# Delta rule block inverse: the four lower levels computed for the even block columns only, packed to 32 columns

## Chip, cores and metric

One NeuronCore of a Trainium2 chip runs the whole program. The metric is device time in microseconds (us) of one execution. The kernel before takes 2286.87 us, the median of three runs.

## What is computed

The reference applies two transformer blocks to a tensor `x` of 256 tokens by 2048 channels. The first block mixes tokens with a multiscale pool and with an RWKV-7 recurrence, which is a delta rule:

```python
def step(S, inp):
    r_t, w_t, k_t, v_t, a_t, b_t = inp
    sa = jnp.einsum('bhij,bhj->bhi', S, a_t)
    S = S * w_t[:, :, None, :] + sa[..., None] * b_t[:, :, None, :] + v_t[..., None] * k_t[:, :, None, :]
    y = jnp.einsum('bhij,bhj->bhi', S, r_t)
    return S, y
...
k = k * (1.0 + (a - 1.0) * k_a.astype(f32))
r_h, k_h, v_h, a_h = hs(r), hs(k), hs(v), hs(a)
y = wkv7_scan(r_h, hs(decay), k_h, v_h, -kk, kk * a_h)
```

There are 16 heads of size 64. The block goes on with `w_out`, a wide MLP (8192) and a gated embedding. The second block has a gated linear attention, a sparse attention and a SwiGLU MLP. All of it is float32.

## The kernel before

The kernel takes the recurrence in chunks of C = 64 tokens, NCH = 4 of them. Inside a chunk the dependence of each token on the earlier ones is a strictly triangular 64x64 matrix G for each head. The kernel needs the inverse of identity minus G for 16 heads x 4 chunks = 64 small matrices. Two heads share the 128 partitions: HM = 8 pairs m, with head e of a pair on partitions 0 to 63 or 64 to 127.

The inverse is built by doubling. It starts from 2x2 diagonal blocks (`level1`). Then, for block size b = 2, 4, 8, 16 (`LEVELS`, line 35), pairs of neighbouring b-blocks are joined into 2b-blocks. The last size, 32, is done apart, by `corner_group` (line 948). Names of this stage:

- `Di` (line 270) holds the inverse so far, `DTi` (line 269) its transpose.
- `Fi` (line 271) holds the intermediate product under a mask. The mask `levels` (line 57) keeps only entries whose block row is odd and whose block column is the even one just before it.
- A level works in four groups g of two pairs each. A group has 2 x 4 x 2 = 16 products of 64x64 matrices (`inverse_group`, line 931). They fill one PSUM bank as 8 x 64 columns, the two heads of a pair in the two halves of the partitions.

One level lv runs like this. TensorE makes G x Di for the four groups into the banks `INV` (line 966, `f_ready`). VectorE multiplies each bank with the mask into `Fi` (line 2377, `f_masked`). TensorE makes D x Fi for the four groups, with DTi as the stationary operand, into banks 4 and 5 in turn (line 975, `df_ready`). VectorE adds each bank to Di (line 2360, `d_added`), and turns Di into DTi (line 2309, `dt_turned`). The next level's first products wait for `d_added`, its second products for `dt_turned`. With two banks for the second products, group 2 waits until group 0 has been added.

Every engine runs its own program in order, so the order around the stage is the order of the source. Between the two sets of products TensorE has `pool_half` (line 920): 24 products of 128x256 for another part of the model, recorded at line 673 in the helper `three`. Its first use here, `pool_half(0)`, waits for a weight tile that VectorE splits in `low1(7, 2)` (line 2205). Between masks and additions VectorE has one long operation per level: `low1(7, 3)` at level 0, `mask_copied` (line 2350) at level 1, `low1(8, 0)` at level 2, `mask_copied` at level 3. A `low1` is a subtraction over 128x2048 elements.

After the levels come the corner products, a turn of v (line 944), two more `pool_half`, the copies of the corners (lines 2397 and 2402), and the sequential scan over the chunks (lines 1004 to 1041).

A float32 product stands in the trace as two pairs of LDWEIGHTS and MATMUL. So 4 levels x 8 groups x 16 products = 512 calls are 1024 records of line 937.

Of the kernel before, what the change touches and what calls it, by code (L numbers as in the profile page):

```python
# [14 lines left out]
ALU = mybir.AluOpType  # L15
# [3 lines left out]
P = 128  # L19
T = 256  # L20
# [9 lines left out]
HM = RW // P  # L30
C = 64
NCH = T // C
KAPPA = float(np.exp(-0.5))
GN_EPS = 64e-5
LEVELS = (2, 4, 8, 16, 32)
# [86 lines left out]
def build(nc, inp, consts, out):  # L122
# [46 lines left out]
    PS = ctx.enter_context(nc.psum_tensor("PS", [P, 8, 512], F32))  # L169

    S = {n: ctx.enter_context(nc.semaphore(n)) for n in SIGNALS.split()}
# [8 lines left out]
    def split(v, dims):  # L180
        if len(dims) == 2:
            return v.rearrange("p (a b) -> p a b", a=dims[0])
        if len(dims) == 3:
            return v.rearrange("p (a b c) -> p a b c", a=dims[0], b=dims[1])
        if len(dims) == 4:
            return v.rearrange("p (a b c d) -> p a b c d", a=dims[0], b=dims[1], c=dims[2])
        return v

    def area(at, *dims):
        n = int(np.prod(dims))  # L190
        assert at + n <= NA, (at, dims)
        return split(arena[:, at:at + n], dims)

    def over(ap, n):

        return ap.unsqueeze(1).broadcast_to([ap.shape[0], n, ap.shape[1]])
# [49 lines left out]
    B32 = C // 2  # L246
# [11 lines left out]
    B = 27 * ZW  # L258
# [9 lines left out]
    G = area(B, HM, 2, NCH, P)  # L268
    DTi = area(AR_AT + 4096, HM, NCH, C)
    Di = area(AR_AT + 6144, HM, NCH, C)  # L270
    Fi = area(B + 4 * 2048, HM, NCH, C)
    UVa = [area(AR_AT + 6144, 2, HM, 2, C), area(B + 4 * 2048, 2, HM, 2, C)]

    def UV(c):
# [23 lines left out]
    INV = (2, 3, 0, 1)  # L298
# [18 lines left out]
    GT = area(B + 2048, HM, T)  # L317

    XN1 = area(B, TT, D)

    gain1 = small[:, 64:80]
    RB1 = area(AR_AT + 5632, T)
# [328 lines left out]
    def _(pe):  # L651
# [227 lines left out]
        for g in range(2 * (NCH - 1)):  # L879
            c, m0 = g // 2, g % 2 * 4  # L880
            if g >= 4:
                pe.wait_ge(S["bk_copied" if g % 2 else "bk_taken"], (g - 2) // 2)
            for m in range(4):
                mm = pe.transpose(PS[:, 4 + g % 4, m * P:(m + 1) * P], BK[:, m0 + m, c, :], ident)
# [35 lines left out]
        def pool_half(x):  # L920

            pool_tile(2 + x // 2, x % 2)
# [8 lines left out]
        def inverse_group(g, bank, lhs, rhs):  # L931
            for m in range(2 * g, 2 * g + 2):
                for c in range(NCH):
                    for e in range(2):
                        h = HALF[e]
                        at = (m % 2 * NCH + c) * C
                        mm = pe.matmul(PS[h, bank, at:at + C], lhs(h, m, c, e), rhs(h, m, c, e), start=True, stop=True)  # L937
            return mm

        def turn_v(c):  # L940
# [17 lines left out]
        for lv in range(len(LEVELS) - 1):  # L958
            for g in range(4):
                if lv == 0:  # L960
                    pe.wait_ge(S["score_masked"], 2 * HM - 3 + g)
                    pe.wait_ge(S["score_copied"], 2 * g + 2)
                    pe.wait_ge(S["d_ready"], g + 1)
                else:
                    pe.wait_ge(S["d_added"], 4 * (lv - 1) + g + 1)
                inverse_group(g, INV[g], lambda h, m, c, e: G[h, m, e, c, 0:C], lambda h, m, c, e: Di[h, m, c, :])\
                    .then_inc(S["f_ready"], 1)
            pool_half(lv)
            for g in range(4):
                pe.wait_ge(S["f_masked"], 4 * lv + g + 1)  # L970
                if lv:
                    pe.wait_ge(S["dt_turned"], 4 * (lv - 1) + g + 1)
                if g >= 2:
                    pe.wait_ge(S["d_added"], 4 * lv + g - 1)
                inverse_group(g, 4 + g % 2, lambda h, m, c, e: DTi[h, m, c, :], lambda h, m, c, e: Fi[h, m, c, :])\
                    .then_inc(S["df_ready"], 1)

        for g in range(2):
# [34 lines left out]
        for c in range(NCH):  # L1013
# [4 lines left out]
            for m in range(HM):  # L1018
                for e in range(2):
                    mm = pe.matmul(PS[HALF[e], 0, m * C:(m + 1) * C], G[:, m, e, c, 0:C], UV(c)[:, m, e, :],  # L1020
                                   start=True, stop=True)
# [7 lines left out]
            for m in range(HM):  # L1029
                for e in range(2):  # L1030
                    mm = pe.matmul(PS[HALF[e], 1, m * C:(m + 1) * C], DTi[HALF[e], m, c, :], ZSB[HALF[e], m, :],
                                   start=True, stop=True)
# [5 lines left out]
            if c < NCH - 1:  # L1038
                for m in range(HM):
                    for e in range(2):  # L1040
                        mm = pe.matmul(PS[HALF[e], 2, m * C:(m + 1) * C], BKtok(c)[:, m, e * C:(e + 1) * C],
                                       UV(c)[:, m, e, :], start=True, stop=True)
# [34 lines left out]
        for t in range(TT):  # L1077
            pe.wait_ge(S["gate_copied"], t + 1)
            pe.wait_ge(S["yn_ready"], t + 1)
            for m in range(HM):  # L1080
                mm = pe.transpose(PS[:, 4 + 2 * t + m // 4, m % 4 * P:(m % 4 + 1) * P], Ytok[:, t, m * P:(m + 1) * P], ident)
# [85 lines left out]
        for n in range(N_KCVC, N_GOQ):  # L1167
# [3 lines left out]
            if n == N_KSVS:  # L1171
                pe.wait_ge(S["w_low"], NARROW)
                for k in range(KT):
                    mm = three(PS[0:SWM, 4, 0:T], (SWH[:, k, :], SW[:, k, :]), (woven(XH[:, k, :]), woven(actT[:, k, :])),
                               k == 0, k == KT - 1)
# [3 lines left out]
        for h in range(GH):  # L1179
            mm = pe.matmul(PS[:, 6 + h // 2, h % 2 * T:(h % 2 + 1) * T], GW2[:, h * P:(h + 1) * P], LR, start=True, stop=True)  # L1180
        mm.then_inc(S["low_rank"], 1)
        for t in range(TT):
            mm = pe.transpose(PS[:, 5, t * 24:t * 24 + 24], LRG[32:SWM, t * P:(t + 1) * P], ident[32:SWM, 32:SWM])
# [84 lines left out]
        for i in range(2):  # L1268
            mm = pe.matmul(PS[:, 4 + i, :], con("ones"), KSQ[:, 2 * i:2 * i + 2, :].rearrange("p a b -> p (a b)"),
                           start=True, stop=True)  # L1270
# [7 lines left out]
        for t in range(TT):  # L1278
            for h in range(GH):
                mm = pe.transpose(PS[:, 4 + t, h * P:(h + 1) * P], K4[:, h, t * P:(t + 1) * P], ident)  # L1280
# [59 lines left out]
        for i in range(2):  # L1340
            mm = pe.transpose(PS[:, 2, i * CB:(i + 1) * CB], PTAB[i], ident[0:CB, 0:CB])
# [60 lines left out]
        for kv in range(KVH):  # L1402
            mm = pe.matmul(PS[0:NB, 3, P + kv * DH:P + (kv + 1) * DH], HID[1][:, kv * NB:(kv + 1) * NB], CW2[1], start=True, stop=True)
# [64 lines left out]
        for c in range(4):  # L1468
            n = N_REST2 + c // 2
            if c >= 2:  # L1470
                pe.wait_ge(S["sum_step"], SUM["out2"] + c - 1)
            for j in (2 * (c % 2), 2 * (c % 2) + 1):
                pe.wait_ge(S["w_low"], split_count(n, j))
                wh, wl = (a.rearrange("p (k n) -> p k n", k=4) for a in (high_home(n, i, j), unit_at(n % 2, j)))
                for k in range(4):
                    for t in range(TT):
                        x, tok = 8 + j % 2 * 4 + k, slice(t * P, (t + 1) * P)
                        mm = three(pair[c % 2][:, t, :], (XH2[:, x, tok], actT[:, x, tok]),
                                   (woven(wh[:, k, :]), woven(wl[:, k, :])), x == 8, x == KT - 1)
# [37 lines left out]
    def _(act):  # L1517
# [68 lines left out]
        def first_squares(c):  # L1586

            act.wait_ge(S[X_LOADED[c]], 16)
            act.activation(XN1[:, 0, CW * c:CW * (c + 1)], xs[:, 0, CW * c:CW * (c + 1)], ACT.Square,
                           accum_out=chunk_sums[:, 0, c:c + 1]).then_inc(S["chunk_summed"], 1)  # L1590
# [11 lines left out]
        for h in range(2):  # L1602
            act.wait_ge(S["n1_dve"], 6 + h)
            copy(r32(XH1[h]), XN1[:, h, :].rearrange("p (k t) -> p k t", k=8)).then_inc(S["x1_high"], 1)

# [481 lines left out]
    def _(v):  # L2087
# [88 lines left out]
        def first_squares(c):  # L2176

            v.wait_ge(S[X_LOADED[c]], 16)
            v.tensor_tensor_reduce(out=XN1[:, 1, CW * c:CW * (c + 1)], in0=xs[:, 1, CW * c:CW * (c + 1)],
                                   in1=xs[:, 1, CW * c:CW * (c + 1)], scale=1.0, scalar=0.0, op0=ALU.mult, op1=ALU.add,  # L2180
# [15 lines left out]
        for h in range(2):  # L2196
            v.tensor_tensor(XN1[:, h, :].rearrange("p (k t) -> p k t", k=8), actT[:, 8 * h:8 * h + 8, :], over(RB1, 8),
                            ALU.mult).then_inc(S["n1_dve"], 1)
# [8 lines left out]
        for h in range(2):  # L2207
            v.wait_ge(S["x1_high"], h + 1)
            v.tensor_tensor(r32(XL1[h]), XN1[:, h, :].rearrange("p (k t) -> p k t", k=8), high_of(XH1[h]), ALU.subtract)\
                .then_inc(S["x1_low"], 1)  # L2210
# [82 lines left out]
        for e in range(2):  # L2293
            h = HALF[e]
# [21 lines left out]
        for g in range(2 * HM):  # L2316
            m, e = g // 2, g % 2
# [34 lines left out]
        def eight(a, g):  # L2352
            return a[:, 2 * g:2 * g + 2].rearrange("p m c j -> p (m c) j")

        def bank8(b):
            return PS[:, b, :].rearrange("p (q j) -> p q j", q=8)

        def block_added(lv, g):
            v.wait_ge(S["df_ready"], 4 * lv + g + 1)
            v.tensor_tensor(eight(Di, g), bank8(4 + g % 2), eight(Di, g), ALU.add).then_inc(S["d_added"], 1)  # L2360

        def block_turned(lv, g):
            v.wait_ge(S["d_added"], 4 * lv + g + 1)
# [9 lines left out]
        for lv in range(len(LEVELS) - 1):  # L2373
            mask = con("levels")[:, lv * C:(lv + 1) * C]
            for g in range(4):
                v.wait_ge(S["f_ready"], 4 * lv + g + 1)
                v.tensor_tensor(eight(Fi, g), bank8(INV[g]), over(mask, 8), ALU.mult).then_inc(S["f_masked"], 1)
            if lv == 0:
                low1(7, 3)
            elif lv == 1:  # L2380
                mask_copied(slice(0, P), slice(C, P))
            elif lv == 2:
                low1(8, 0)
            else:
                mask_copied(LO, slice(0, C))
            block_added(lv, 0)
            block_added(lv, 1)
            block_turned(lv, 0)
            block_added(lv, 2)
            block_turned(lv, 1)  # L2390
            block_added(lv, 3)
            block_turned(lv, 2)
            block_turned(lv, 3)
# [91 lines left out]
        for i in range(F1_PARTS):  # L2485
            for c in range(8):
                n = N_F1 + c
# [33 lines left out]
        for c in range(4):  # L2521
            n, r = N_GATE + c, xs[:, :, columns(c)]
# [42 lines left out]
        for c in range(4):  # L2565
            n = N_GLA + c
# [537 lines left out]
```

## Time and profile before

| | |
|---|---|
| three runs, us | 2286.87, 2286.2, 2287.71 |
| median, us | 2286.87 |
| profiled execution, span from first to last instruction, us | 2284.1 |
| TensorE matmul busy | 2262.9 us (99%) |
| TensorE weight load busy | 2054.8 us (90%) |
| VectorE busy | 1453.5 us (64%) |
| ScalarE busy | 981.0 us (43%) |
| GpSimd busy | 169.3 us (7%) |
| granted TensorE clock | 0.999 of full speed |

The profile gives one execution by its span alone. The median of the runs is 2.8 us above it, which is time before the first and after the last instruction together with the scatter between executions. In the rows below, PE is TensorE's matmuls, PEld its weight loads, DVE is VectorE, ACT is ScalarE, POOL is GpSimd. A matmul's duration reaches from its start to its modelled end and overlaps with the next ones, so that the rate of a burst is read from where it starts, where the next line starts and how many records lie between.

### The profile page before, as it was taken

The numbers are of one execution on the slowest core, as the hardware profiler recorded it, in microseconds if no ns is written. First come the engines' busy times: TensorE is split into PE (matmuls) and PEld (weight loads), VectorE is DVE, ScalarE is ACT, GpSimd is POOL, SyncE is SP. The second block draws the span as 40 slices with busy tenths as digits, with TensorE's granted clock in tenths as the row PEclk, the third lists the DMA queues.
The fourth block names the chain that finished last, engine by engine and source line by source line (L and its number), as shares of the span: only waits on it lengthen the run. The fifth ranks groups of instructions, "written<-read, shape, count | busy, mean of one in ns | idle before, by whom it ended". The sixth has DMA issues, their size and how long they took to land.

```text
span 2284.1 us, 34500 instructions
## 1 busy us (share of the span) xinstructions
PE 2262.9 (99%) x15676; PEld 2054.8 (90%) x15676; DVE 1453.5 (64%) x1214; ACT 981.0 (43%) x931; POOL 169.3 (7%) x136
## 2 busy tenths in 40 slices
PE   9999999999999999999999999999999999999999
PEld 8998988998988988988889999888998998999898
DVE  6699676664665665665558559686655665565564
ACT  5653355433333333344544364475343433433442
POOL 1004110110110110110000000100000000011000
PEclk9999999999999999999999999999999999999999
DMA  8553166656665656666556655345555655665644
GB/s 252 174 163 90 34 238 199 207 192 211 194 215 190 212 193 205 200 231 209 175 179 190 190 183 151 117 142 184 193 194 199 224 187 184 221 211 176 227 160 147
DMA packets 335306, 425.06 MB, mean 186 GB/s; under 512 B 4521, under 2 KB 249625, under 8 KB 334777
## 3 DMA queue, kind: packets, MB, share of 16 engines
q1 hardware_dynamic: 333465, 418.50, 56.2%
q0 software_dynamic: 1552, 4.23, 0.6%
q8 instruction: 123, 2.02, 0.4%
q14 instruction: 22, 0.18, 0.0%
q10 hardware_dynamic: 144, 0.13, 0.0%
HBM read 420.75 MB, written 2.10 MB: 185 GB/s over the span
## 4 chain that ended last, share of the span: by engine, by line
PE 94%; DVE 5%; ACT 1%; issue 0%; DMA 0%; DVEq 0%; SPq 0%; ACTq 0%
PE PS L673 51%; PE PS L719 23%; PE PS L721 11%; PE PS L937 1%; DVE ring_r L2205 1%; PE PS L718 1%; PE PS L738 1%; PE PS L1129 1%; PE PS L856 0%; PE PS L1200 0%; ACT arena_r L1527 0%; PE PS L1010 0%; PE PS L1065 0%; PE PS L1057 0%; PE PS L1319 0%
## 5 line engine op out<-in xcount | busy, mean ns | idle before, releaser
L1527 ACT ACTIVATE arena_r<-ring 128x2048 fp32r<-128x2048 f32 (+1 forms) x394 | 689.9, 1759 | 934.2 <-PE PS L673 536.1
L2147 DVE TENSOR_TENSOR ring_r<-ring,arena_r 128x2048 fp32r<-128x2048 f32 x316 | 721.5, 2290 | 489.9 <-ACT arena_r L1527 489.9
L719 PE MATMUL PS<-arena_r,arena_r 128*128 128x512 f32 x2432 | 789.7, 382 | 0.0
L673 PE MATMUL PS<-arena_r,arena_r 128*128 128x512 f32 (+2 forms) x2128 | 707.6, 346 | 0.9 <-DVE actT_r L2138 0.7
L721 PE MATMUL PS<-arena_r,ring_r 128*128 128x256 f32 x2280 | 621.5, 273 | 0.0
L673 PE MATMUL PS<-ring_r,arena_r 128*128 128x512 f32 (+1 forms) x1504 | 523.3, 361 | 1.2 <-DVE ring_r L2205 1.2
L719 PEld LDWEIGHTS PS<-arena_r,arena_r 128*128 128x128 f32 x2432 | 449.1, 189 | 56.2
L673 PE MATMUL PS<-arena_r,actT_r 128*128 128x512 f32 (+1 forms) x1184 | 442.1, 373 | 0.0
L721 PEld LDWEIGHTS PS<-arena_r,ring_r 128*128 128x128 f32 x2280 | 437.4, 192 | 4.0
L673 PEld LDWEIGHTS PS<-arena_r,arena_r 128*128 128x128 f32 (+1 forms) x2128 | 401.5, 189 | 42.9 <-issue 4.8
L673 PEld LDWEIGHTS PS<-ring_r,arena_r 128*128 128x128 f32 x1504 | 277.4, 190 | 35.7 <-issue 3.1
L673 PEld LDWEIGHTS PS<-arena_r,actT_r 128*128 128x128 f32 x1184 | 224.0, 189 | 30.0
L673 PE MATMUL PS<-actT_r,arena_r 128*128 128x256 f32 (+1 forms) x656 | 180.4, 275 | 0.0
L673 PE MATMUL PS<-arena_r,ring_r 128*128 128x256 f32 x640 | 176.0, 275 | 0.0
L673 PE MATMUL PS<-ring_r,actT_r 128*128 128x256 f32 x832 | 143.3, 278 | 1.6 <-DVE ring_r L2205 1.6
L673 PE MATMUL PS<-ring_r,ring_r 128*128 128x256 f32 x512 | 140.8, 275 | 0.0
L673 PEld LDWEIGHTS PS<-ring_r,actT_r 128*128 128x128 f32 x832 | 126.4, 192 | 4.2 <-DVE ring_r L2205 2.1
L673 PEld LDWEIGHTS PS<-actT_r,arena_r 128*128 128x128 f32 (+1 forms) x656 | 124.9, 190 | 0.3 <-issue 0.2
L673 PEld LDWEIGHTS PS<-arena_r,ring_r 128*128 128x128 f32 x640 | 122.9, 192 | 0.0
L3036 POOL TENSOR_TENSOR arena_r<-arena,cst 128x1024 fp32r<-128x1024 f32 x16 | 62.0, 3876 | 612.9 <-DVE arena L2509 612.9
L2540 DVE TENSOR_TENSOR ring_r<-ring,arena_r 128x1024 fp32r<-128x1024 f32 x56 | 68.4, 1235 | 50.4 <-ACT arena_r L1527 50.3
L673 PEld LDWEIGHTS PS<-ring_r,ring_r 128*128 128x128 f32 x512 | 98.3, 192 | 0.0
(381 smaller groups left out, 1639.1 us busy)
## 6 DMA issues: line engine op xcount, KB each, us to landing
ring<-in_w_ffn_up SPq DMA_DIRECT2D x32, 2048.0 KB, 9.4
ring<-in_w_ffn_down SPq DMA_DIRECT2D x32, 2048.0 KB, 7.9
ring<-in_w_in SPq DMA_DIRECT2D x22, 2048.0 KB, 8.2
ring<-in_w_gate SPq DMA_DIRECT2D x22, 2048.0 KB, 8.2
ring<-in_w_up SPq DMA_DIRECT2D x22, 2048.0 KB, 8.2
ring<-in_w_in SPq DMA_DIRECT2D x32, 1024.0 KB, 5.4
ring<-in_w_out SPq DMA_DIRECT2D x16, 2048.0 KB, 8.8
ring<-in_w_down SPq DMA_DIRECT2D x12, 2048.0 KB, 8.1
```

Of the source, the lines that this page charges most:

```text
L673: mm = pe.matmul(dst, r32(w, early)[rows], r32(x, early)[rows], start=first and q == 0, stop=last and q == 2)
L718: pe.matmul(dst[:, 0:T], r32(wl[:, k, c]), r32(high), start=False, stop=False)
L719: mm = pe.matmul(dst, r32(wh[:, k, c]), r32(beside(high, low)), start=x == 0, stop=x == KT - 1)
L721: mm = pe.matmul(dst[:, 0:T], r32(wl[:, k, c]), r32(high), start=False, stop=False)
L738: mm = pe.transpose(PS[:, 8 - banks + j % banks, q * T + t * P:q * T + (t + 1) * P], xs[:, t, k * P:(k + 1) * P], ident)
L937: mm = pe.matmul(PS[h, bank, at:at + C], lhs(h, m, c, e), rhs(h, m, c, e), start=True, stop=True)
L1129: mm = pe.matmul(PS[:, 4 + t, :], pT[:, k, t * P:(t + 1) * P], pproj[:, c, k, :], start=(k == 0), stop=(k == 1))
L1527: return act.activation(dst, src, ACT.Copy, scale=scale)
L2147: v.tensor_tensor(r32(u), u, high_of(high_home(n, i, j)), ALU.subtract).then_inc(S["w_low"], counts(units, j))
L2205: v.tensor_tensor(r32(w), w, high_of(high_at(u), True), ALU.subtract).then_inc(S["in_low"], 1)
L2540: v.tensor_tensor(r32(u), u, high_of(HIH[q % 4]), ALU.subtract).then_inc(S["w_low"], 1)
L3036: pool.tensor_tensor(r32(XD[:, 4 * c:4 * c + 4]), RQ[c % 2], one, ALU.mult).then_inc(S["ffn1_high"], 1)
```

## The change

The mask of a level leaves nothing in the odd block columns. The changed kernel therefore computes only the even block columns of both products, 32 of 64, and packs them beside each other:

- The moving operand of the first products is a strided view of Di: blocks of b columns, every other one (`even`). Its stationary operand, G, stays 64x64.
- The masks read 8 x 32 columns of PSUM and write a packed `FE` of 32 columns a matrix at the place of `Fi`.
- The second products have `FE` as the moving operand, 32 columns; the stationary operand DTi stays 64x64.
- The additions change the even block columns of Di alone.

The number of instructions, their order on every engine, and all waits stay as they were. The turns of Di into DTi, the pool products and the long VectorE operations are unchanged, as is the corner step.

```diff
+    FE = area(B + 4 * 2048, HM, NCH, C // 2)
...
+    def even(ap, b):
+
+        names = {2: "p", 3: "p q", 4: "p m c"}[len(ap.shape)]
+        return ap.rearrange(f"{names} (n s b) -> {names} n s b", s=2, b=b)[..., 0, :]
...
-                        at = (m % 2 * NCH + c) * C
-                        mm = pe.matmul(PS[h, bank, at:at + C], lhs(h, m, c, e), rhs(h, m, c, e), start=True, stop=True)
+                        at = (m % 2 * NCH + c) * B32
+                        mm = pe.matmul(PS[h, bank, at:at + B32], lhs(h, m, c, e), rhs(h, m, c, e), start=True, stop=True)
...
-                inverse_group(g, INV[g], lambda h, m, c, e: G[h, m, e, c, 0:C], lambda h, m, c, e: Di[h, m, c, :])\
+                inverse_group(g, INV[g], lambda h, m, c, e: G[h, m, e, c, 0:C],
+                              lambda h, m, c, e: even(Di[h, m, c, :], LEVELS[lv]))\
                     .then_inc(S["f_ready"], 1)
...
-                inverse_group(g, 4 + g % 2, lambda h, m, c, e: DTi[h, m, c, :], lambda h, m, c, e: Fi[h, m, c, :])\
+                inverse_group(g, 4 + g % 2, lambda h, m, c, e: DTi[h, m, c, :], lambda h, m, c, e: FE[h, m, c, :])\
                     .then_inc(S["df_ready"], 1)
...
+        def even8(b, lv):
+            return PS[:, b, 0:T].rearrange("p (q n b) -> p q n b", q=8, b=LEVELS[lv])
+
         def block_added(lv, g):
             v.wait_ge(S["df_ready"], 4 * lv + g + 1)
-            v.tensor_tensor(eight(Di, g), bank8(4 + g % 2), eight(Di, g), ALU.add).then_inc(S["d_added"], 1)
+            d = even(eight(Di, g), LEVELS[lv])
+            v.tensor_tensor(d, even8(4 + g % 2, lv), d, ALU.add).then_inc(S["d_added"], 1)
...
-                v.tensor_tensor(eight(Fi, g), bank8(INV[g]), over(mask, 8), ALU.mult).then_inc(S["f_masked"], 1)
+                v.tensor_tensor(eight(FE, g).rearrange("p q (n b) -> p q n b", b=LEVELS[lv]), even8(INV[g], lv),
+                                even(mask, LEVELS[lv]).unsqueeze(1).broadcast_to([P, 8, B32 // LEVELS[lv], LEVELS[lv]]),
+                                ALU.mult).then_inc(S["f_masked"], 1)
```

## Rows read from the trace of the kernel before

**Rows 1.** The page: busy time, share and instructions of each engine.

```profile
PE 2262.9 (99%) x15676; PEld 2054.8 (90%) x15676; DVE 1453.5 (64%) x1214; ACT 981.0 (43%) x931; POOL 169.3 (7%) x136
```

**Rows 2.** Busy time by stretch: us, then us busy of each engine, clock, DMA.

```profile
200.00:247.00 47.00, 44.46 (x1155) 42.81 (x1154) 42.46 (x57) 6.55 (x6) 11.71 (x16) 1.00 0.26 70
247.00:260.00 13.00, 11.78 (x338) 11.30 (x337) 9.75 (x14) 6.28 (x6) 0.00 (x0) 1.00 0.03 6
```

**Rows 3.** Chain of waits over the stage: start us, us, what.

```profile
203.29 2.25 DVE ring_r L2205
205.53 2.39 DVE arena L2377 x4
207.93 2.20 DVE ring_r L2205
210.13 0.61 DVE arena L2360
210.74 0.14 issue
210.88 5.82 PE PS L937 x192
...
226.03 0.84 issue
...
256.29 0.68 DVE arena L2402
```

**Rows 4.** PE in order of time, stage: start us, us, instruction, [idle before, releaser].

```profile
205.59 0.49 PE L673 MATMUL PS<-ring_r,actT_r 128*128 128x256 f32 x2 [0.93 <-DVE ring_r L2205]
...
208.47 2.08 PE L937 MATMUL PS<-arena 64*64 64x64 f32 x64
210.88 5.82 PE L937 MATMUL PS<-arena 64*64 64x64 f32 x192 [0.33 <-DVE arena L2360]
...
231.23 7.85 PE L937 MATMUL PS<-arena 64*64 64x64 f32 x256
239.00 0.49 PE L673 MATMUL PS<-ring_r,actT_r 128*128 128x256 f32 x2
...
255.04 2.21 PE L955 MATMUL PS<-arena 32*32 32x32 f32 x128
257.18 0.38 PE L673 MATMUL PS<-ring_r,actT_r 128*128 128x256 f32 x1
```

**Rows 5.** PE in order of time, later stages with 128-column weights and few moving columns.

```profile
1412.94 1.84 PE L1216 MATMUL PS<-cst,arena 128*128 128x1 f32 x16
1414.64 0.36 PE L673 MATMUL PS<-arena_r,arena_r 128*128 128x256 f32 x1
...
1417.40 1.04 PE L1280 MATMUL PS<-cst,arena 128*128 128x128 f32 x8
1418.28 0.28 PE L1216 MATMUL PS<-cst,arena 128*128 128x1 f32 x2
```

**Rows 6.** Groups by line, PEld: names, shapes, count, busy us, mean ns, idle before.

```profile
L937 PEld LDWEIGHTS PS<-arena 64*64 64x64 f32 x1024 | 30.9, 134 | 2.4 <-issue 1.6
L955 PEld LDWEIGHTS PS<-arena 32*32 32x32 f32 x256 | 4.3, 106 | 1.0 <-issue 0.8
L1216 PEld LDWEIGHTS PS<-cst,arena 128*128 128x128 f32 x32 | 3.7, 192 | 0.0
```

**Rows 7.** One line's instructions, DVE: min/median/max ns, first and last start, forms.

```profile
L2360 DVE TENSOR_TENSOR arena<-PS,arena x16: 650/679/692, 210.0 to 246.4; 128x512 f32<-128x512 f32 x16
...
L2330 DVE TENSOR_TENSOR arena<-PS,cst x8: 375/404/406, 179.5 to 201.0; 64x256 f32<-64x256 f32 x8
...
L2213 DVE TENSOR_TENSOR arena<-PS,arena x1: 418/418/418, 27.6 to 27.6; 128x256 f32<-128x256 f32 x1
```

**Rows 8.** Waits from 200 to 250 us: who waited for whom, us, times, longest.

```profile
DVE arena L2360 <- PE PS L937: 3.6, 6, 1.1
...
PE PS L937 <- DVE arena L2360: 0.3, 1, 0.3
```

**Rows 9.** DVE in order of time: the last level's end.

```profile
246.43 0.65 DVE L2360 TENSOR_TENSOR arena<-PS,arena 128x512 f32<-128x512 f32 x1
247.01 1.28 DVE L2309 STREAM_TRANSPOSE arena<-arena 128x512 f32<-128x512 f32 x2
```

## Prediction

> **What bounds the kernel now.** I read the page first: TensorE is busy 99% of the span [rows 1], so only what shortens TensorE's own program, or a wait in it, can shorten the kernel. Busy time by stretch comes next. The inverse is a small stretch, 200 to 247 us, and in it TensorE is busy 44.5 of 47 us and VectorE 42.5 [rows 2]. Both are nearly full, so the chain of waits has to say which one sets the pace. It runs on VectorE up to 210.74 us: a weight split, the four masks of level 0, another split, one addition [rows 3]. From 210.88 us it stays on TensorE until 256.29 us, where the corner copies take over [rows 3]. The waits say the same. From 200 to 250 us TensorE's products waited for an addition once, 0.3 us, while the additions waited for products six times, 3.6 us [rows 8]. So the stage is VectorE's for its first level and TensorE's for the other three. A saving on VectorE counts before 210.88 us only; a saving on TensorE counts wherever it does not end in a wait.
>
> **What one product costs, and what of it the change halves.** This is the term that decides. The level from 231.23 us has 256 records and the next line starts at 239.00 us: 7.77 us / 256 = 30.35 ns a record [rows 4]. Products of the two heads use different halves of the array and run in turn, so within one half a record comes every 60.7 ns. In that time two things happen side by side: 64 weight columns are loaded and 64 moving columns are streamed. The change halves the second and leaves the first. The rows of this stage cannot tell which of them sets 60.7 ns, because they are equally wide in it. The corner products do not help either: at 16.7 ns a record (128 of them in the 2.14 us from 255.04 us to the next line) they are nearly twice as fast, but both their weights and their moving part are 32 columns wide [rows 4].
>
> Rows from later in the program separate the two. Line 1216 multiplies 128 weight columns with one single moving column: sixteen records from 1412.94 to 1414.64 us, 106.3 ns each. Line 1280 has the same width of weights and 128 moving columns: eight records from 1417.40 to 1418.28 us, 110 ns each [rows 5]. Moving 1 column in place of 128 saves 3.7 ns of 110, or 3.4%. With fewer moving than weight columns, the weight load sets the pace. The loads' own durations fit: 106, 134 and 192 ns for 32, 64 and 128 columns [rows 6], a slope of 0.88 to 0.91 ns a column, so some 56 ns of a 64-column load grow with its width. That is nearly all of the 60.7 ns.
>
> **The sum, part by part.**
>
> *Products.* I take the share that rows 5 show: 30.35 x 106.3 / 110 = 29.3 ns, about 1.0 ns saved a record. Of the 1024 records the first 128 (level 0, first products) end before TensorE has to wait for a weight split anyway, 0.93 us up to 205.59 us [rows 4]; what they save only lengthens that wait. That leaves 896 records, all on the path: 896 x 1.0 = **0.9 us**. Lower end of the saving: 0, if the load alone sets the rate. Upper end: a half-wide load at half of line 1216's 106.3 ns, 53.2 ns in one half of the array, 26.6 ns a record, 896 x 3.8 = 3.4 us. I stay near the lower end, because rows 5 are the only ones that change the moving width and keep the weights'; the other end takes the load to be as fast in half an array as its width alone would make it.
> The Trainium skill, "TensorE: Matmul & The Clock Gate", section "LDWEIGHTS (loading the stationary operand)", says that a load takes its number of columns divided by 1.2, in ns, whatever the contraction. By it 64 columns are 53.3 ns, 26.7 ns a record, and an estimate of the saving is 3.3 us where my sum has 0.9. The trace bears the rule's form out (length by columns), and shows 60.7 ns where the rule alone has 53.3.
>
> *Masks and additions, level 0.* A bank of 128x512 costs 0.60 us in the chain (2.39 / 4) and 0.61 us for an addition [rows 3]. The nearest rows with 256 elements and a PSUM operand are 375 to 418 ns long, against 650 to 692 ns for 512 [rows 7]: about 0.28 us less each. Four masks and an addition bring VectorE forward by 1.4 us, but TensorE had idled only 0.33 us for it, and behind the wait stands its own burst of 64 records. They start at 208.47 us; at 30.35 ns they would be followed at 210.41 us, not 210.88: **0.5 us** saved. The other 0.9 us of VectorE's gain are slack. Strided access costs nothing here by rows 7: line 2213 reads both operands with a stride of 128 columns, and 418 ns is its time for 256 elements.
>
> *Masks and additions, levels 1 to 3.* Twelve of each by 0.28 us are 6.7 us of VectorE time. They save nothing: TensorE's products cover them, and VectorE already waits for TensorE there [rows 8]. If the products were much faster, VectorE would be late next (first rival).
>
> *Waits, DMAs, order.* None is added or moved. The turns, the pool products and the long VectorE operations stay. What TensorE gains here passes to the end, since it is busy 99% of the span [rows 1] and its transfers are released by its own progress.
>
> **Sum:** 0.9 + 0.5 = 1.4 us off a span of 2284.1 us, giving 2282.7 us. The median of the runs stands 2.8 us above that span, and 2286.87 - 1.4 = **2285.5 us**. A difference of 0.2%, 4.6 us, is about what a measurement of this kernel can tell from no change, so I forecast no change.
>
> **Rivals.**
>
> *The moving columns set the pace.* Then a record with 32 moving columns comes at the corner's 16.7 ns [rows 4], in spite of 64-column weights. TensorE would save 896 x 13.65 = 12.2 us, a level being 256 x 16.7 ns + 2.9 us of pool products = 7.2 us. VectorE then becomes the bound: 8 x 0.32 us for masks and additions, 2.2 us for the long operation [rows 3] and 4 x 0.62 us for the turns (two in a row take 1.28 us [rows 9]) make 7.3 us a level, some 7.5 us with handovers. Four levels from 205.5 us, without the last two turns (1.2 us), end at 234.3 us, where the last addition now ends at 247.0 us [rows 9]. Less a microsecond for stalls like the 0.84 us at 226.03 us [rows 3], the kernel would take about 2275.4 us, 11.5 us less. For it: weights and moving part are equally wide in every product of this stage, so nothing in the stage contradicts it. Against it: line 1216, where one moving column still costs 106.3 ns.
>
> *The array is fed so little that its clock falls.* Half of the columns streamed are gone for 45 us. If the granted clock dropped from full speed, 2.4 GHz, to 1.2 GHz over one level with its pool products (7.8 + 2.9 us), those would take 10.7 us longer, less my 1.4 us: 2296.2 us, slower. It decides from 12 us at the lower clock: half of that is lost, and less 1.4 us it passes 4.6 us. For it: this is the only stretch in which TensorE's work per time is cut. Against it: the clock stayed at 1.00 in the stretch with the corner products, which stream 32 columns over a block of 32 rows at a time, and with PE idle 1.2 of 13 us [rows 2].
>
> *The change does not do what it says.* The short strided runs of Di (two columns of four at level 0) could be read no faster than all 64. That gives nothing where the load sets the pace anyway: 2286.4 us, from the 0.5 us alone. It is inside my forecast.
>
> **How the numbers follow.** Weight load sets the pace (with the last case in it): 0.84, 2285.5 us. Moving columns set it: 0.13, 2275.4 us. Clock falls: 0.03, 2296 us. The first case ranges from 0.5 + 3.4 = 3.9 us saved, 2283.0 us, up to nothing saved and the spread of the runs above their median (0.8 us), 2287.7 us. The other two hold 0.16, so the range is the first case's own: 2283.0 to 2287.7 us. The first case lies within 0.2%, the second is faster by more, the third slower by more: 0.13, 0.84, 0.03.
>
> **What would show it.** In the changed kernel's trace the 256 records of a middle level should still take 7.4 to 7.8 us from their start to the next line, though each matmul's own duration is shorter, and LDWEIGHTS should keep its mean of 134 ns. The masks and additions should have means of 0.37 to 0.42 us. The wait of 0.33 us before the level-0 products should be gone, and VectorE should wait for line 937's successor by some 6 us more in all. Everything behind 260 us should be the same, earlier by 1.4 us. The prediction is wrong if a record comes much faster than 27 ns, or if VectorE takes the chain in the middle levels, or if the clock column shows less than 1.00 between 200 and 250 us.

## The result: 3 us slower, and the profile after

Over 21 runs each, the changed kernel takes 2289.33 us (median, 2287.39 to 2293.34) and the kernel before 2286.33 us (2285.68 to 2289.48). The ratio is 1.0013, with a 95% interval of 1.0007 to 1.0019: 3 us, or 0.13%, slower. That is inside the 0.2% of the forecast "no change", but the sign is the other one, and the time lies outside the forecast range.

The profiled execution has a span of 2287.3 us, 3.2 us above that of the kernel before. The page shows TensorE 4 us busier and VectorE 9 us less busy than [rows 1]:

```profile
PE 2267.0 (99%) x15676; PEld 2059.1 (90%) x15676; DVE 1444.9 (63%) x1214; ACT 981.6 (43%) x931; POOL 169.5 (7%) x136
```

Where the time is lost stands in the stage itself. This is the chain of waits of the changed kernel (start us, us, what); L943 are the products of the inverse, L679 the pool products, L961 the corner, L950 the turn of v, L2415 the copies of the corners:

```profile
205.96 2.94 PE PS L679 x24
208.91 7.58 PE PS L943 x256
...
225.66 1.04 issue
226.70 1.52 PE PS L943 x45
228.23 4.50 PE PS L679 x24
232.73 7.58 PE PS L943 x256
240.31 2.88 PE PS L679 x24
243.19 3.85 PE PS L943 x128
247.04 0.62 PE PS L961 x30
247.66 1.09 issue
248.75 2.68 PE PS L961 x57
251.43 3.61 PE PS L950 x64
255.04 3.27 PE PS L679 x24
258.31 1.15 PE PS L961 x64
```

Compare the rows of 24 pool products (L679): the same 24 instructions take 2.94 and 2.88 us in two of the rows shown, 4.50 us and 3.27 us in the two others. They were not touched by the change. The busy time by stretch (us, us busy of PE, PEld, DVE, ACT, POOL, granted clock, DMA share, GB/s) tells why:

```profile
200.00:228.00 28.00, 25.91 (x695) 25.21 (x695) 22.01 (x37) 4.37 (x4) 9.08 (x12) 1.00 0.30 79
228.00:232.00 4.00, 4.00 (x26) 3.96 (x24) 2.62 (x2) 0.00 (x0) 0.00 (x0) 0.57 0.00 0
232.00:248.00 16.00, 15.66 (x445) 15.22 (x444) 10.83 (x20) 2.18 (x2) 2.95 (x5) 1.00 0.24 65
248.00:256.00 8.00, 7.25 (x167) 7.07 (x167) 5.78 (x7) 4.48 (x3) 0.00 (x0) 0.57 0.05 12
256.00:262.00 6.00, 6.00 (x163) 5.84 (x162) 2.42 (x4) 1.82 (x4) 0.00 (x0) 1.00 0.01 3
```

The granted clock is 0.57 in two stretches, where the kernel before had 1.00 [rows 2]. A mean of 0.57 means most of the stretch at 1.2 GHz. In finer stretches it is 0.50 from 229 to 231 us and from 249 to 254 us:

```profile
229.00:231.00 2.00, 2.00 (x11) 0.50 0.00 0
...
249.00:250.00 1.00, 1.00 (x49) 0.50 0.13 30
```

Ahead of each fall TensorE ran narrow products and then stood idle for about a microsecond, the "issue" pieces of the chain at 225.66 and 247.66 us. The Trainium skill, "TensorE: Matmul & The Clock Gate", section "What's actually happening", says that the array's clock is throttled by default and that activity releases it. The rows agree in kind: less streamed, less clock.

**The account.** From the start of the first products to the first work behind the corner copies the changed kernel needs 63.49 us (200.81 to 264.30 us), the kernel before 60.65 us (200.45 to 261.10 us), 2.84 us more. Burst by burst, from start to the next line's start:

| piece | us more (+) or less (-) |
|---|---|
| first product burst behind the level-0 wait: 7.58 us, was 8.15 with the wait | -0.57 |
| the three other bursts of the inverse, without their gaps | -0.57 |
| pool products at the lower clock: 4.50 and 3.27 us, were 2.88 | +2.01 |
| corner products and turn of v, without their gaps | +2.28 |
| idle gaps without visible cause: 1.04 + 1.09, were 0.84 + 0.69 + 0.92 | -0.32 |
| sum | +2.83 |

So the change gave 1.14 us, the gaps 0.32 us, and the clock took 4.29 us back. The clock was low for about 10 us in all: 0.57 over 4 us and over 8 us.

The 21 executions say the same by themselves. Those with a mean granted clock of 0.998 have spans of 2285.5 to 2287.6 us, those with 0.997 have 2287.0 to 2288.7 us, the two with 0.995 have 2291.1 and 2291.5 us. None of the 21 has more than 0.998.

### The profile page after: what moved, and what is told of

The parts are those of the page before. It is cut to its first block, busy times and chain, and to the rows that moved or that the text cites. A ratio compares the mean times of both kernels' runs of the same rounds, so it can differ in the third digit from the quotient of the medians.

```text
span 2287.3 us, 34500 instructions
## 1 busy us (share of the span) xinstructions
PE 2267.0 (99%) x15676; PEld 2059.1 (90%) x15676; DVE 1444.9 (63%) x1214; ACT 981.6 (43%) x931; POOL 169.5 (7%) x136
## 4 chain that ended last, share of the span: by engine, by line
PE 94%; DVE 4%; ACT 1%; issue 0%; DVEq 0%; POOL 0%; ACTq 0%; POOLq 0%
PE PS L679 51%; PE PS L725 23%; PE PS L727 11%; PE PS L943 1%; DVE ring_r L2212 1%; PE PS L724 1%; PE PS L744 1%; PE PS L1136 1%; PE PS L862 0%; PE PS L1207 0%; ACT arena_r L1534 0%; PE PS L1017 0%; PE PS L1072 0%; PE PS L1064 0%; PE PS L1326 0%
## 5 line engine op out<-in xcount | busy, mean ns | idle before, releaser
L679 PE MATMUL PS<-arena_r,arena_r 128*128 128x512 f32 (+2 forms) x2128 | 707.5, 346 | 0.9 <-DVE actT_r L2145 0.7
L679 PE MATMUL PS<-ring_r,arena_r 128*128 128x512 f32 (+1 forms) x1504 | 523.2, 361 | 1.2 <-DVE ring_r L2212 1.2
L679 PE MATMUL PS<-arena_r,actT_r 128*128 128x512 f32 (+1 forms) x1184 | 442.1, 373 | 0.0
L679 PEld LDWEIGHTS PS<-arena_r,arena_r 128*128 128x128 f32 (+1 forms) x2128 | 401.4, 189 | 43.0 <-issue 4.8
L679 PEld LDWEIGHTS PS<-ring_r,arena_r 128*128 128x128 f32 x1504 | 277.4, 190 | 35.8 <-issue 3.1
L679 PEld LDWEIGHTS PS<-arena_r,actT_r 128*128 128x128 f32 x1184 | 224.0, 189 | 30.0
L679 PE MATMUL PS<-actT_r,arena_r 128*128 128x256 f32 (+1 forms) x656 | 180.4, 275 | 0.0
L679 PE MATMUL PS<-arena_r,ring_r 128*128 128x256 f32 x640 | 176.0, 275 | 0.0
L679 PE MATMUL PS<-ring_r,actT_r 128*128 128x256 f32 x832 | 145.2, 280 | 1.7 <-DVE ring_r L2212 1.7
L679 PE MATMUL PS<-ring_r,ring_r 128*128 128x256 f32 x512 | 141.8, 277 | 0.0
L679 PEld LDWEIGHTS PS<-ring_r,actT_r 128*128 128x128 f32 x832 | 128.1, 194 | 4.2 <-DVE ring_r L2212 2.1
L679 PEld LDWEIGHTS PS<-actT_r,arena_r 128*128 128x128 f32 (+1 forms) x656 | 124.9, 190 | 0.3 <-issue 0.2
L679 PEld LDWEIGHTS PS<-arena_r,ring_r 128*128 128x128 f32 x640 | 122.9, 192 | 0.0
L679 PEld LDWEIGHTS PS<-ring_r,ring_r 128*128 128x128 f32 x512 | 99.2, 194 | 0.0
```

Source lines behind the costliest of these rows:

```text
L679: mm = pe.matmul(dst, r32(w, early)[rows], r32(x, early)[rows], start=first and q == 0, stop=last and q == 2)
```

## Experiments

Two theories stood at the start. **Clock:** TensorE, fed half of the columns, is granted a lower clock for some microseconds, and work that was not changed runs slow in it. **Access:** the short strided reads of Di or the packed masks and additions cost the time, and the clock is a bystander.

### Feed 64 columns again, keep everything else

```diff
-                        at = (m % 2 * NCH + c) * B32
-                        mm = pe.matmul(PS[h, bank, at:at + B32], lhs(h, m, c, e), rhs(h, m, c, e), start=True, stop=True)
+                        n = C if wide else B32
+                        at = (m % 2 * NCH + c) * n
+                        x = rhs(h, m, c, e)
+                        mm = pe.matmul(PS[h, bank, at:at + n], lhs(h, m, c, e), twice(x) if wide else x, start=True, stop=True)
...
+WIDE1, WIDE2 = (0, 1, 2, 3), (0, 1, 2, 3)
```

`twice` reads the 32 needed columns two times over; VectorE works on the first 32. `WIDE1` and `WIDE2` are the levels at which this is done for the first and for the second products.

> The changed kernel with the 32 needed columns of the moving operand of both products streamed twice, so that each product streams 64 columns again; masks, additions and packing stay those of the change. Clock theory (the change loses because TensorE, fed half as many columns, is granted 1.2 GHz for some microseconds): clock column 1.00 from 200 to 260 us, a level's 256 records back at 7.8 us, and the level-0 wait of 0.33 us still gone, so 0.5 us less than the kernel before, about 2285.9 us. Rival (the short strided reads of Di, or the packed masks and additions of VectorE, cost the time): both are still there, the strided reads twice over, so it stays 3 us above the kernel before, 2289.3 us.

Measured: 2286.44 us (11 runs), ratio 1.0001 (0.9992 to 1.0009). Its 200 to 262 us by stretch (us, PE busy, clock, DMA):

```profile
228.00:232.00 4.00, 4.00 (x63) 1.00 0.00 0
232.00:240.00 8.00, 8.00 (x247) 1.00 0.02 4
...
248.00:252.00 4.00, 3.35 (x134) 1.00 0.04 8
```

The strided reads are there twice, the packed masks and additions are there, and the 3 us are gone with the clock at 1.00. As the cause of the 3 us, the access theory falls. Against the kernel before nothing is gained either: I had expected 0.5 us for the level-0 wait. TensorE's bursts in order of time (L950 the inverse, L680 the pool products, L968 the corner) say why:

```profile
208.41 8.22 PE L950 MATMUL PS<-arena 64*64 64x64 f32 x256
216.56 0.49 PE L680 MATMUL PS<-ring_r,actT_r 128*128 128x256 f32 x2
...
231.20 7.68 PE L950 MATMUL PS<-arena 64*64 64x64 f32 x256
238.82 0.49 PE L680 MATMUL PS<-ring_r,actT_r 128*128 128x256 f32 x2
...
241.69 3.95 PE L950 MATMUL PS<-arena 64*64 64x64 f32 x128
245.57 0.69 PE L968 MATMUL PS<-arena 32*32 32x32 f32 x30
```

The first burst has no wait in it and still takes 8.15 us, as long as in the kernel before with its wait. Its second half are the first products of level 1, which read runs of four columns of Di twice over. Read record by record, the trace has them 32.6 ns apart within a group of 32. In the changed kernel the same products with 32 columns come every 28.4 ns. So doubled short runs do cost time, about 0.5 us here, and use up what the level-0 wait gave back; read once, as in the changed kernel, they cost nothing. The two other bursts take 7.62 and 3.88 us, against 7.58 and 3.85 us with 32 columns.

### Feed 64 columns in one of the two products

```diff
-WIDE1, WIDE2 = (0, 1, 2, 3), (0, 1, 2, 3)
+WIDE1, WIDE2 = (), (0, 1, 2, 3)
```

> Only the second products (D x F) stream 64 columns again, the first stream 32. Clock theory: half of the cut is given back, so one of the two falls of the clock (228.5 to 232 us, 249 to 256 us) or both should go; 2286 to 2288 us. If the strided reads of Di by the first products were the cause, all of the loss would stay: 2289.3 us.

```diff
-WIDE1, WIDE2 = (0, 1, 2, 3), (0, 1, 2, 3)
+WIDE1, WIDE2 = (0, 1, 2, 3), ()
```

> Only the first products (G x D) stream 64 columns again, the second stream 32. Clock theory: as with the second products alone, 2286 to 2288 us, since only the amount streamed counts and not which product streams it. A cause in the packed FE as moving operand would keep all of the loss: 2289.3 us.

Measured: 2287.24 us (ratio 1.0005, 0.9996 to 1.0014) with the second products wide, 2287.55 us (1.0004, 0.9995 to 1.0013) with the first ones wide. Both are between the two ends and within the error of either, so the halves can't be told apart by time. The mean clocks say that either half alone costs clock: none of these 22 executions has 1.000, where 5 of 11 have it with both products wide. In the profiled executions the clock held at 228 to 232 us and fell near 249 us with the first products wide, and fell at both places with the second ones wide. Each of the two is the slowest of its 11 executions (2288.29 and 2291.02 us), so this does not show which half matters more. By stretch (us, PE busy, clock, DMA), first products wide:

```profile
228.00:232.00 4.00, 4.00 (x64) 1.00 0.00 0
...
248.00:252.00 4.00, 3.71 (x116) 0.62 0.02 6
```

and second products wide:

```profile
228.00:232.00 4.00, 4.00 (x32) 0.50 0.00 0
```

### Narrow products at level 3 only

```diff
-WIDE1, WIDE2 = (0, 1, 2, 3), (0, 1, 2, 3)
+WIDE1, WIDE2 = (0, 1, 2), (0, 1, 2)
```

> Levels 0 to 2 stream 64 columns again, level 3 alone streams 32. Clock theory: the fall from 228.5 to 232 us goes with the narrow products before it; the fall from 249 us may stay, because narrow products, an idle gap and the corner products come before it. About 2286 us if both go, 2287.5 us if the second stays. Rival (cost per narrow product): a quarter of the loss stays in every run, 2286.9 us with the clock at 1.00.

Measured: 2284.61 us (ratio 0.9992, 0.9983 to 1.0001), below both kernels and 1.4 us below the lowest time that I had expected. It was run again:

> The run with narrow products at level 3 alone, once more, to see whether its 2284.6 us repeats: clock full, 2284.3 to 2285 us. If that was an accident of one call, 2286 us or more.

Measured: 2284.64 us (11 runs), ratio 0.9990 (0.9981 to 0.9999). It repeats. The mean clock was 1.000 in 10 of these 11 executions. PE in order of time in the first of the two runs (start us, us, what, idle before):

```profile
227.30 1.58 PE L950 MATMUL PS<-arena 64*64 64x64 f32 x45 [1.22 <-issue]
231.69 7.66 PE L950 MATMUL PS<-arena 64*64 64x64 f32 x256
242.15 3.92 PE L950 MATMUL PS<-arena 64*64 64x32 f32 x128
246.00 2.21 PE L968 MATMUL PS<-arena 32*32 32x32 f32 x128
```

Two things set it apart: the clock holds, and the gap at the first corner products is absent (128 records in one piece, where the kernel before had 0.69 us of idleness among them). Gaps from 200 to 260 us are 1.75 us in all in this run, 1.5 us in its repetition, 2.45 us in the kernel before. Why that gap is absent is not shown.

### Narrow products at levels 2 and 3

```diff
-WIDE1, WIDE2 = (0, 1, 2, 3), (0, 1, 2, 3)
+WIDE1, WIDE2 = (0, 1), (0, 1)
```

> Levels 0 and 1 stream 64 columns, levels 2 and 3 stream 32. Twice the narrow products of the run with level 3 alone. Clock theory: between that run (2284.6 us, clock full in nearly all executions) and the changed kernel (2289.3 us): falls in some executions, 2285 to 2288 us. If narrow products gave a gain by themselves, it should be more than with level 3 alone: below 2284.6 us.

Measured: 2289.74 us (11 runs, 2288.80 to 2290.98), ratio 1.0014 (1.0006 to 1.0023). My expectation of something in between was wrong: half of the narrow products cost as much as all of them. The loss is not a price per narrow product. Its profiled execution has the clock low in the same two places, and once more from 192 to 195 us (0.50), ahead of any product of the inverse; that fall can't come from the narrow products. The two places:

```profile
228.00:232.00 4.00, 4.00 (x57) 0.69 0.02 4
...
252.00:256.00 4.00, 4.00 (x92) 0.50 0.01 4
```

### Half of the moving columns again

```diff
-                        mm = pe.matmul(PS[h, bank, at:at + B32], lhs(h, m, c, e), rhs(h, m, c, e), start=True, stop=True)
+                        mm = pe.matmul(PS[h, bank, at:at + 16], lhs(h, m, c, e), rhs(h, m, c, e), start=True, stop=True)
...
-                              lambda h, m, c, e: even(Di[h, m, c, :], LEVELS[lv]))\
+                              lambda h, m, c, e: even(Di[h, m, c, 0:B32], LEVELS[lv]))\
...
-                inverse_group(g, 4 + g % 2, lambda h, m, c, e: DTi[h, m, c, :], lambda h, m, c, e: FE[h, m, c, :])\
+                inverse_group(g, 4 + g % 2, lambda h, m, c, e: DTi[h, m, c, :], lambda h, m, c, e: FE[h, m, c, 0:16])\
```

> The changed kernel with 16 moving columns in place of 32 in both products; half of the needed columns is left out, and masks and additions read zeros from SBUF in place of PSUM, in the same shapes. Theory that the 64-column weight load sets the pace: a level's 256 records still take 7.6 us (29.6 ns each) where the clock is full, nothing is gained by the product, and the clock falls at least as long as in the changed kernel: 2289 us or more, up to 2293 us. Rival (moving columns still count): 256 records in less than 7 us.

Measured: 2303.44 us (4 runs), ratio 1.0072 (1.0059 to 1.0085), 17 us above the kernel before and more than I had expected. The clock was low from the first level on:

```profile
200.00:210.00 10.00, 9.38 (x154) 0.70 0.39 107
210.00:220.00 10.00, 10.00 (x226) 0.67 0.01 2
220.00:228.00 8.00, 8.00 (x78) 0.51 0.01 3
```

The edit has a side effect: its masks and additions put zeros into `FE`, so that the second products stream zeros. They can't be the cause of the first fall. The clock is at 0.51 from 204 to 205 us, and the first mask starts at 205.53 us. For the later falls this run doesn't separate the zeros from the width.

The last product burst fell into a stretch at full clock (1.00 from 256 to 262 us; it began at 256.37 us). Order of time, with the next line:

```profile
256.37 3.91 PE L943 MATMUL PS<-arena 64*64 64x16 f32 x128
260.21 0.69 PE L961 MATMUL PS<-arena 32*32 32x32 f32 x30
```

128 records in 3.84 us are 30.0 ns each, against 3.85 us with 32 columns. Halving the moving columns once more gave nothing at full clock, and the clock was much worse. Both halves of the explanation are in this run, the second with the zeros as a reservation.

### Half of the weight columns as well

```diff
-                        mm = pe.matmul(PS[h, bank, at:at + B32], lhs(h, m, c, e), rhs(h, m, c, e), start=True, stop=True)
+                        mm = pe.matmul(PS[EARLIER[e], bank, at:at + B32], lhs(h, m, c, e)[:, 0:B32], rhs(h, m, c, e), start=True, stop=True)
```

> The changed kernel with 32 weight columns in place of 64 as well (half of the output rows is left out; masks and additions read zeros from SBUF, in the same shapes). Load theory: the pace falls to that of the corner products, about 16.7 ns a record at full clock, 128 records in 2.1 us; VectorE then sets the pace of the levels at some 7.5 us each. At full clock the kernel would take about 2276 us; with TensorE idle or fed narrow products most of the time the clock should fall for longer than in the changed kernel, and give some of it back: 2276 to 2284 us. Rival (a floor per product of about 25 to 30 ns, whatever its width): 29.6 ns a record and no gain.

Measured: 2284.84 us (10 runs), ratio 0.9992 (0.9983 to 1.0001). PE in order of time:

```profile
218.99 1.20 PE L943 MATMUL PS<-arena 64*32 64x32 f32 x64
220.67 2.82 PE L943 MATMUL PS<-arena 64*32 64x32 f32 x147 [0.48 <-DVE arena L2372]
226.43 1.09 PE L943 MATMUL PS<-arena 64*32 64x32 f32 x45 [2.93 <-issue]
```

64 records in 1.20 us are under 19 ns, about 16 ns without the last one's own duration: the pace nearly halves with the width of the weights. Since 16, 32 and 64 moving columns had left it alone, the weight load sets it, in this stage too, and the rival's floor of 25 to 30 ns does not exist. But the kernel gains 1.2 us, not 10, and ends just outside the 2276 to 2284 us that I had expected. The waits of its PE say where the rest went:

```profile
PE PS L943 <- issue: 5.0, 3, 2.9
PE PS L961 <- issue: 1.9, 1, 1.9
```

6.9 us are gaps in which TensorE waits for nothing that the profile shows. They were 1.5 us at these lines in the kernel before. Together with a clock of 0.83 from 200 to 210 us, 0.70 from 228 to 232 us and 0.64 from 248 to 252 us they eat the gain: an estimate from these numbers is 5.4 us for the longer gaps and some 4 us for the clock (half of the time at 1.2 GHz).

### Spread the wide products

```diff
-        def pool_half(x):
+        def pool_half(x, ks=range(8)):
...
-            pool_half(lv)
+            pool_half(lv, range(0, 4))
             for g in range(4):
...
                     .then_inc(S["df_ready"], 1)
+            pool_half(lv, range(4, 8))
```

Twelve of a level's 24 pool products go behind its second products, so that narrow products stand at most 128 records in a row, not 256. This edit was put on the changed kernel, on the one that streams 64 columns, on the kernel before, and on the one with level 3 narrow.

> The changed kernel (narrow products) with the 24 wide pool products of each level split: 12 between first and second products as before, 12 behind the second products. The longest stretch of narrow products alone halves from 7.6 to 3.9 us. Clock theory: the falls become shorter or rarer; with none, the kernel takes 2286 us (0.5 us less for the wait, up to 0.5 us more for four more changes between narrow and wide products). Rival (only the total amount streamed matters): the same falls as in the changed kernel, 2289 us.

Measured: 2285.08 us (median of 12), ratio 1.0005 (0.9994 to 1.0016), but with a scatter from 2284.07 to 2297.49 us. The seven executions below 2286 us have a mean clock of 0.999 to 1.000, the five above 2287 us one of 0.993 to 0.998. Against the changed kernel, where all 21 are at 0.998 or less, spreading makes the falls rarer and does not prevent them.

> Both products stream 64 columns (the 32 needed twice), masks and additions packed, and the pool products of each level split in two as in the run with narrow products. Clock theory: the clock stays full in nearly every execution, so the slow executions of the split narrow kernel (up to 2297 us) are gone, and the median is near its fast ones: 2284 to 2286 us. If instead the split itself made the scatter, executions above 2290 us would remain.

Measured: 2285.23 us, ratio 0.9992 (0.9983 to 1.0001), all 11 executions between 2284.60 and 2285.85 us with a clock of 0.999 to 1.000. The only edit against the split kernel just above is that the 32 columns are streamed twice, and the scatter is gone.

> The kernel before with nothing but its pool products split in two at each level. It tells whether the split gains by itself, since in the split narrow kernel TensorE's idle gaps for no visible reason (0.84, 0.69 and 0.92 us in the kernel before) were gone. If they go here too: up to 2 us less, 2284.5 to 2286 us. If the split only adds changes between narrow and wide products: 2286.5 to 2287 us.

Measured: 2286.92 us, ratio 1.0000 (0.9992 to 1.0009). The gaps shrink to 0.2 us, but VectorE's addition is now late for longer, as its waits show, where [rows 8] had 0.3 us:

```profile
PE PS L937 <- DVE arena L2361: 1.7, 1, 1.7
...
PE PS L944 <- issue: 0.2, 1, 0.2
```

So with unpacked masks the split moves the wait; the packed masks and additions are what makes it pay (0.4 us of wait in the wide run above). The slowest of the 11 packed executions, 2285.85 us, is below the fastest of the 11 unpacked ones, 2286.26 us.

> Level 3 alone narrow, and the pool products split in two at each level. If the gains of the two add up (idle gaps gone, wait gone, clock full): 2284 us or less; if the narrow level makes the clock fall in some executions, a scatter up to 2288 us.

Measured: 2285.15 us, ratio 0.9994 (0.9985 to 1.0003). The gains don't add up: 0.5 us more than level 3 narrow without the split.

## Why the prediction was wrong

**What bounds the kernel: right in the main.** Level 0 is VectorE's, the rest TensorE's, but for a short wait for VectorE in each level (next point). In the changed kernel the chain leaves VectorE at 205.92 us and stays on TensorE up to the corner copies.

**Products, 0.9 us: the number was nearly met, the reason was not; this is luck.** 29.3 ns a record was forecast from [rows 5]; the two bursts of 256 records take 7.58 us, 29.6 ns, against 30.35 ns [rows 4], and the three bursts behind the first gave 0.57 us. But the kernel that streams 64 columns with packed masks and additions takes 7.62 us for such a burst. So of the 0.19 us that a burst gained, 0.15 us came without any narrowing of the products. Read record by record, the step within a group of 32 is 28.5 ns with 64 and with 32 moving columns: the width itself gave next to nothing, the lower end of my range. What went away is a wait that I had put at nothing. Between the second and the third group of the second products of levels 1 to 3, 0.17 us pass from one record's start to the next in the kernel before, and 0.05 us in the changed kernel. The third group waits for the addition that frees its bank. At level 3 that addition is this one; it ends at 243.77 us, and the third group starts at 243.91 us, the same 0.14 us later as at 210.74 us in [rows 3]:

```profile
243.08 0.69 DVE L2360 TENSOR_TENSOR arena<-PS,arena 128x512 f32<-128x512 f32 x1 [0.88 <-PE PS L937]
```

An addition of 0.4 us ends in time. The waits of [rows 8] do not list these short waits of TensorE, and "they save nothing" for the masks and additions of levels 1 to 3 was wrong by about 0.35 us (3 x 0.12 us).

That the weight load sets the pace is borne out all the same, by the runs with 16 moving columns (no gain) and with 32 weight columns (about 16 ns a record). The rule of the Trainium skill, "TensorE: Matmul & The Clock Gate", section "LDWEIGHTS (loading the stationary operand)", 53.3 ns for 64 columns, would have had 26.7 ns a record; its form holds, and the stage stays 2.9 ns a record above it.

**Level-0 wait, 0.5 us: right in the trace.** The first burst runs in one piece, in 7.58 instead of 8.15 us. Record by record, 0.50 us of that lie between the last start of its second group and the first of its third, 0.55 us before and 0.05 us now.

**Masks and additions, their length: right; that they were wholly hidden: not quite, as said above.** They have medians of 412 to 422 ns, and VectorE waits for products longer than in [rows 8]:

```profile
DVE arena L2371 <- PE PS L943: 8.1, 8, 2.9
DVE arena L2388 <- PE PS L943: 4.3, 6, 1.8
```

That is 12.4 us against 4.3 us (3.6 us, and 0.7 us for the masks), 8 us more where I had said 6 us.

**The step that failed is the second rival's chance.** "The clock stayed at 1.00 in the stretch with the corner products ... and with PE idle 1.2 of 13 us" was my reason to give the clock 3%. That stretch followed 45 us of products of 64 columns. I took it as evidence for a stretch that follows 45 us of products of 32, and so the sum has no term for the clock. The clock falls exactly there now: corner products and turn of v run at 0.57. It also falls from 228 to 232 us, which is the sign that I had named for being wrong, a clock below 1.00 between 200 and 250 us. The price was mis-sized too, in the other direction: I priced one whole level at the lower clock, 10.7 us lost; the clock was low for about 10 us, the falls hit pool products, corner and turn of v, and they cost 4.3 us. Less the 1.14 us of the change (1.4 forecast) and 0.3 us of shorter gaps this is the +2.8 us of the stage. The range I gave took none of it in. The base of the forecast was 0.5 us too high as well: the median of three runs was 2286.87 us, that of 21 is 2286.33 us. The first rival, moving columns at 16.7 ns a record, fell with the changed kernel's own 29.6 ns.

**Open.** What the gaps without visible cause are was not settled. They differ between kernels by up to a microsecond or two and decide at this scale which one looks best. Also open is why narrow products at levels 2 and 3 cost over 3 us and those at level 3 alone nothing. In the profiled executions with 32 moving columns somewhere and the pool products in one piece, each fall in the stage came with narrow products and a gap before it (with the second products wide, the last narrow product of the inverse lies 9 us before the second fall), and the two with level 3 alone narrow had no gap at the corner and no fall there. That is a pattern of single executions, not a test, and with 16 columns the clock fell without a gap.

## What to carry to other kernels

Before halving the moving side of a small matmul, look at how wide its weights are: with 64 weight columns, 64, 32 and 16 moving columns all came at about 30 ns a record here at full clock. Such columns are free here, and taking them out can cost TensorE its clock in work that was not touched, so price unchanged neighbours at the lower clock before calling a change neutral. And when a rate comes out as forecast, compare it with a run that changes only the other half of the edit: here the rate was met by the shorter additions and not by the narrower products. The best version here keeps 64 columns at levels 0 to 2 and narrow products at level 3: 2284.6 us, 1.8 us below the kernel before (ratio 0.9990, 0.9981 to 0.9999, in the repetition) and 4.7 us below the change.

## What the runs showed of the hardware that I had not expected

- Columns that cost no time still count for the clock: 64, 32 and 16 moving columns at the same pace at full clock gave 2286.4, 2289.3 and 2303.4 us (the last with zeros in the second products).
- Moving columns read twice over in runs of four were slower than read once: 32.6 against 28.4 ns a record at level 1.
- The fall also comes with TensorE listed as busy: 4.00 of 4.00 us in the stretch from 228 to 232 us, in which the clock was 0.57. A busy share near one is no sign of full clock.
- Even the kernel before has executions with a mean clock of 0.997 to 0.999 and up to 5 us above its median. The wide kernel with split pool products had none above 2285.85 us.
